# Gate rows made by transposing repeated columns, a new order of the first units, nine warm-up products, and a delta-rule inverse in 64-column tiles

## The reference

```python
def gated_delta_rule(q, k, v, g, beta):      # chunks of 64 tokens
    gc = jnp.cumsum(g, axis=-1)
    decay = jnp.exp(jnp.where(incl, gc[..., :, None] - gc[..., None, :], -jnp.inf))
    kb = k * beta
    low = jnp.where(strict, jnp.einsum("bhnid,bhnjd->bhnij", kb, k) * decay, 0.0)
    rhs = jnp.concatenate([v * beta, kb * jnp.exp(gc)[..., None]], axis=-1)
    sol = lax.linalg.triangular_solve(low + jnp.eye(c), rhs, left_side=True, lower=True, unit_diagonal=True)
...
def _fox_attention(q, k, v, f_pre):
    cum = jnp.cumsum(jax.nn.log_sigmoid(f_pre).transpose(0, 2, 1), axis=-1)
...
    s = s + (cqc[..., None] - cum[:, :, None, :])
```

## Time and profile before

| | us |
|---|---|
| median of three runs | 1081.33 (1081.12 to 1082.15) |
| the profiled execution, its own time | 1081.43 |
| its span in the trace | 1079.6 |
| PE busy | 1051.2 (97%) |
| DVE busy | 756.2 (70%) |
| ACT busy | 542.3 (50%) |
| POOL busy | 12.6 (1%) |

### The profile page before, as it was taken

How to read it: one execution, slowest core, us unless ns; L and a number is a source line. 1 busy time by engine, 2 the same in 40 slices (tenths; PEclk the granted TensorE clock), 3 DMA queues, 4 the chain that set the end, 5 groups by cost and what they waited for, 6 DMA issues and landing times.

```text
span 1079.6 us, 19214 instructions
## 1 busy us (share of the span) xinstructions
PE 1051.2 (97%) x7938; PEld 932.7 (86%) x7938; DVE 756.2 (70%) x1051; ACT 542.3 (50%) x601; POOL 12.6 (1%) x13
## 2 busy tenths in 40 slices
PE   9999999999999999999999999989999989999998
PEld 7999999999976798989899877659986659999986
DVE  6989947678458767677777856857797765556535
ACT  5675534563353463547536334576677654353331
POOL 0100000000000000000000000002000000000000
PEclk8999999999999999999999999999999999999999
DMA  8454432334325663425343354776344364545441
GB/s 343 157 180 155 157 118 90 138 125 159 115 79 213 252 239 155 132 104 193 121 157 118 118 200 153 310 291 260 127 156 156 103 243 163 195 172 181 176 163 51
DMA packets 26293, 181.32 MB, mean 168 GB/s; under 512 B 3040, under 2 KB 3296, under 8 KB 4960
## 3 DMA queue, kind: packets, MB, share of 16 engines
q1 hardware_dynamic: 25056, 174.66, 44.1%
q10 hardware_dynamic: 1152, 5.45, 1.2%
HBM read 179.04 MB, written 1.05 MB: 167 GB/s over the span
## 4 chain that ended last, share of the span: by engine, by line
PE 89%; DVE 7%; ACT 2%; issue 1%; DMA 1%; ACTq 0%; DVEq 0%; SPq 0%
PE PS L912 86%; DVE WL L1778 1%; PE PS L1065 1%; PE PS L1143 1%; DVE X L1972 1%; DVE X L1971 1%; DMA RAW<-wst 1%; PE PS L1289 0%; DVE layer_ln L2083 0%; DVE STAT L1953 0%; DVE X L1952 0%; ACT block L1606 0%; DVE X L2264 0%; DVE XTL L1995 0%; DVE layer L2076 0%
## 5 line engine op out<-in xcount | busy, mean ns | idle before, releaser
L912 PE MATMUL PS<-XTH,WH 128*128 128x256 f32 x1392 | 404.4, 291 | 0.7 <-issue 0.5
L912 PE MATMUL PS<-XTH,WL 128*128 128x256 f32 x1392 | 394.5, 283 | 0.0
L912 PE MATMUL PS<-XTL,WH 128*128 128x256 f32 x1392 | 394.4, 283 | 0.0
L1778 DVE TENSOR_TENSOR WL<-RAW,WH 128x2048 fp32r<-128x2048 f32 x138 | 316.9, 2297 | 107.9 <-ACT WH L1368 104.7
L1368 ACT ACTIVATE WH<-RAW 128x2048 fp32r<-128x2048 f32 x138 | 262.7, 1903 | 194.8 <-PE PS L912 191.2
L912 PEld LDWEIGHTS PS<-XTH,WH 128*128 128x128 f32 x1392 | 267.6, 192 | 6.3 <-issue 3.7
L912 PEld LDWEIGHTS PS<-XTL,WH 128*128 128x128 f32 x1392 | 267.7, 192 | 2.8 <-issue 2.6
L912 PEld LDWEIGHTS PS<-XTH,WL 128*128 128x128 f32 x1392 | 267.5, 192 | 0.0
L912 PE MATMUL PS<-WH,YH 128*128 128x512 f32 x224 | 89.6, 400 | 1.1 <-DVE YL L2256 1.1
L912 PE MATMUL PS<-WH,YL 128*128 128x512 f32 x224 | 87.4, 390 | 0.0
L912 PE MATMUL PS<-WL,YH 128*128 128x512 f32 x224 | 87.3, 390 | 0.0
(11 more groups left out here) (295 smaller groups left out, 1178.0 us busy)
## 6 DMA issues: line engine op xcount, KB each, us to landing
RAW<-wst SPq DMA_DIRECT2D x162, 1024.0 KB, 4.9
LNW<-lnrow ACTq DMA_DIRECT2D x3, 1024.0 KB, 6.4
RAW<-wst SPq DMA_DIRECT2D x4, 512.0 KB, 4.8
layer<-xt SPq DMA_DIRECT2D x2, 512.0 KB, 5.8
XR<-x ACTq DMA_DIRECT2D x1, 1024.0 KB, 6.2
out<-X SPq DMA_DIRECT2D x4, 256.0 KB, 2.1
CST<-cst ACTq DMA_DIRECT2D x1, 640.0 KB, 8.9
PT<-pt SPq DMA_DIRECT2D x1, 512.0 KB, 5.6
```

Source lines behind the costliest of these rows:

```text
L912: return pe.matmul(o, lhsT, rhs, start=start, stop=stop)
L1778: tt(WL[:, i % RAW_RING, 0:n], RAW[:, i % RAW_RING, 0:n], as_float(WH[:, k % SPLIT_RING, 0:n]), ALU.subtract).then_inc(vector_done, 1)
```

## The change

1. `gt` is gone. A new step `gcc:g` on PE is the small product with `triu` alone, and DVE's `gcc:g` copies its eight columns to `GCOL`. `gc:g` on PE is now eight transposes of a column of `GCOL` repeated 128 times. `gcc:0` stands right behind `norm:k:0` and waits for DVE's `ba2`; `gcc:1` stands behind `ab:1:0` and claims bank 2.
2. `gsp` is gone. DVE's `gcol` also stores the cumulated columns (`GRC`), and `grow` is 12 and 8 transposes.
3. PE begins with nine warm-up products, `first:k:0:0` and `k:0:0`, and `ba` after them. ACT and DVE split x's first half ahead of the slab's top half.
4. `gp` and `gu` on levels 1 to 6 are two products of 64 output rows in the place of one of 128: 16 PE instructions for 8, in each of the 48 steps.

```diff
 ORDER_T = """
-ba first:k:0:0 k:0:0 first:k:0:1 k:0:1 first:v:0:0 v:0:0 norm:k:0 first:v:0:1 v:0:1 first:q:0:0 q:0:0 first:q:0:1
+first:k:0:0 k:0:0 ba first:k:0:1 k:0:1 first:v:0:0 v:0:0 norm:k:0 gcc:0 first:v:0:1 v:0:1 first:q:0:0 q:0:0 first:q:0:1
...
-ab:1:0 first:zb:1:0 zb:1:0 gc:1 first:zb:1:1 first:ah:1:1 zb:1:1 vtr:1 norm:q:1 first:ac:1:1 ah:1:1 first:az:1:1
+ab:1:0 gcc:1 first:zb:1:0 zb:1:0 gc:1 first:zb:1:1 first:ah:1:1 zb:1:1 vtr:1 norm:q:1 first:ac:1:1 ah:1:1 first:az:1:1
...
-split_top xs:1 split:0:0 xs:0 ba split:1:1 split:2:2 ba1 k:0:0 split:3:3 k:0:1 split:4:4 v:0:0 split:5:5 ba2 norm:k:0
+xs:0 split_top xs:1 split:0:0 split:1:1 ba split:2:2 ba1 k:0:0 split:3:3 k:0:1 split:4:4 v:0:0 split:5:5 ba2 norm:k:0
...
+            def t_gcc(step, g):
+                pe.wait_ge(vector_done, vector_at("ba2"))
+                pe.wait_ge(cst_loaded, 16)
+                mm(PS[:, 2, 0:8], triu, GG[:, g, :]).then_inc(tensor_done, 1)
+
+            def repeated(o, column):
+
+                return pe.transpose(o, column.to_broadcast([P, P]), ident)
+
             def t_gc(step, g):
-                pe.wait_ge(vector_done, vector_at("ba2"))
-                pe.wait_ge(gpsimd_done, gpsimd_at("gt", g))
-                pe.wait_ge(cst_loaded, 16)
-                gt = flat(PM)
-                for i in range(2):
-                    mm(PS[:, i, :], ONES[:], gt[:, i * SLAB:(i + 1) * SLAB])
-                mm(PS[:, 2, 0:8], triu, GG[:, g, :]).then_inc(tensor_done, 1)
+                pe.wait_ge(vector_done, vector_at("gcc", g))
+                for m in range(NT * HG):
+                    last = repeated(PS[:, m // HG, m % HG * P:(m % HG + 1) * P], GCOL[:, m:m + 1])
+                last.then_inc(tensor_done, 1)
...
-                    last = mm(odd(PS[:, c, h * P:(h + 1) * P], i), DL[:, m, :], odd(U[:, m, :], i))
+                    for b in range(2):
+                        r = slice(b * HD, (b + 1) * HD)
+                        last = mm(odd(PS[r, c, h * P:(h + 1) * P], i), DL[:, m, r], odd(U[:, m, :], i))
...
             def t_grow(step, part):
-                pe.wait_ge(vector_done, vector_at("gsp"))
-                pe.wait_ge(gpsimd_done, gpsimd_at("gsp"))
+                pe.wait_ge(vector_done, vector_at("gcol"))
...
-                        o = a * T
-                        mm(PS[:, b, o:o + P], ONES[:], GSP[0][:, j, :])
-                        tot = NLS[:, 0, gate_of(j):gate_of(j) + 1].to_broadcast([P, P])
-                        mm(PS[:, b, o + P:o + T], ONES[:], tot, stop=False)
-                        last = mm(PS[:, b, o + P:o + T], ONES[:], GSP[1][:, j, :], start=False)
+                        for c in range(NT):
+                            o = a * T + c * P
+                            last = repeated(PS[:, b, o:o + P], GRC[:, c, j:j + 1])
...
-            for _ in range(6):
+            for _ in range(9):
                 mm(PS[:, 7, :], ONES[:], ONES[:].unsqueeze(1).to_broadcast([P, 4, P]))
```

More of the change, by code:

```diff
@@ L278, in gdn @@
     def gdn(g):
-        out = [later(step, "gt", g, on="G"),
-               later(step, "gc", g, on="TVS", banks=(0, 1, 2)),
+        out = [later(step, "gcc", g, on="TV", banks=(2,)),
+               later(step, "gc", g, on="TVS", banks=(0, 1)),
                later(step, "gc2", g, on="V"),
@@ L413, in plan @@
     root(0, 0)
-    step("gsp", on="GV")
     feat(2)
@@ L511 @@
 ORDER_S = """
-setup split_top xs:1 split:0:0 xs:0 split:1:1 ba1 split:2:2 split:3:3 k:0:0 split:4:4 k:0:1 split:5:5 ba2 norm:k:0
+setup xs:0 split_top xs:1 split:0:0 split:1:1 ba1 split:2:2 split:3:3 k:0:0 split:4:4 k:0:1 split:5:5 ba2 norm:k:0
 v:0:0 split:6:6 split:7:7 q:0:0 v:0:1 split:8:8 zb:0:0 q:0:1 split:9:9 split:10:10 zb:0:1 gc:0 split:11:11 norm:q:0
@@ L544 @@
 ORDER_V = """
-split_top xs:1 split:0:0 xs:0 ba split:1:1 split:2:2 ba1 k:0:0 split:3:3 k:0:1 split:4:4 v:0:0 split:5:5 ba2 norm:k:0
-split:6:6 q:0:0 split:7:7 v:0:1 q:0:1 split:8:8 gc:0 split:9:9 split:10:10 k:1:0 split:11:11 vtr:0 norm:q:0
+xs:0 split_top xs:1 split:0:0 split:1:1 ba split:2:2 ba1 k:0:0 split:3:3 k:0:1 split:4:4 v:0:0 split:5:5 ba2 norm:k:0
+split:6:6 q:0:0 gcc:0 split:7:7 v:0:1 q:0:1 split:8:8 gc:0 split:9:9 split:10:10 k:1:0 split:11:11 vtr:0 norm:q:0
 split:12:12 k:1:1 gc2:0 gk:0 split:14:14 split:13:13 gkk:0 v:1:0 gp:0:0:1 gp:0:0:0 split:15:15 gu:0:0:1 v:1:1
@@ L551 @@
 split:24:24 gp:0:6:1 ab:0:1 gks:0 gu:0:6:1 split:26:26 split:25:25 ac:1:0 split:27:27 gz:0 gr:0:0 split:28:28 ab:1:0
-gc:1 split:29:29 gc2:1 split:30:30 norm:q:1 vtr:1 gk:1 split:31:31 split:32:32 ac:1:1 gkk:1 split:33:33 ab:1:1
+gcc:1 gc:1 split:29:29 gc2:1 split:30:30 norm:q:1 vtr:1 gk:1 split:31:31 split:32:32 ac:1:1 gkk:1 split:33:33 ab:1:1
 gp:1:0:0 gp:1:0:1 gu:1:0:1 gu:1:0:0 split:34:34 gp:1:1:0 gp:1:1:1 gu:1:1:0 gp:1:2:0 split:35:35 gu:1:1:1 split:36:36
@@ L570 @@
 gate:1:1:1 rmsb:0:1 xt:4:3 xt:4:1 adat:7 xtl:4:2 xtl:4:0 xtl:4:3 xtl:4:1 adat:9 split:88:108 gates:0 split:89:109
-gates:1 ga gb split:90:110 gd split:91:111 qn:1:2 gcol gsp qn:0:0 split:92:112 qn:0:1 split:93:113 qn:0:2 split:95:115
+gates:1 ga gb split:90:110 gd split:91:111 qn:1:2 gcol qn:0:0 split:92:112 qn:0:1 split:93:113 qn:0:2 split:95:115
 split:94:114 feat:3 grow:0 split:96:116 feat:4 mod:1 grow:1 split:97:117 mb split:98:118 qn:1:0 gm score:0 qn:1:1
@@ L585 @@
 ORDER_G = """
-setup gt:0 gt:1 gsp
+setup
 """
@@ L1058, in t_gu @@
                     m = c * HG + h
-                    last = mm(odd(PS[:, 2 + c, h * P:(h + 1) * P], i), XI[:, m, :], odd(PM[:, m, :], i))
+                    for b in range(2):
+                        r = slice(b * HD, (b + 1) * HD)
+                        last = mm(odd(PS[r, 2 + c, h * P:(h + 1) * P], i), XI[:, m, r], odd(PM[:, m, :], i))
                 last.then_inc(tensor_done, 1)
@@ L1839, in v_conv, with v_gcc @@
                 return part
+            def v_gcc(g):
+                dve.wait_ge(tensor_done, tensor_at("gcc", g))
+                if g:
+                    dve.wait_ge(scalar_done, scalar_at("gc", 0))
+                    dve.wait_ge(tensor_done, tensor_at("gc", 0))
+                dve.tensor_copy(GCOL, PS[:, 2, 0:8]).then_inc(vector_done, 1)
             def v_gc(g):
@@ L2316, in g_setup @@
                 pool.memset(EPS[:, 1:2], L2_EPS).then_inc(gpsimd_done, 1)
[L2318 to L2335, removed]
+            parts = {"setup": g_setup}
             mine = 0
```

23 lines of the change are left out of this document (7 added, 16 removed).

## The result

| | before | after |
|---|---|---|
| median, us | 1081.34 (1081.12 to 1082.15) | 1100.75 (1099.76 to 1100.99) |
| ratio, 95% interval | 1 | 1.0176 (1.0159 to 1.0194) |
| span of the profiled execution | 1079.6 | 1099.2 |
| mean granted clock of PE | 0.995 | 0.984 |

What follows compares the result with a forecast made beforehand. PE, busy 1051.2 of 1079.6 us, and its waits were taken as the bound. +10.8 - 0.9 + 4.4 - 4.5 - 4.4 - 0.9 + 3.4 = +7.9 on 1081.43 gave 1089.3 us, range 1083 to 1096.

Steps and rivals of the forecast that it cites:

- The rival in which the waits are covered: ba2 ends before PE is through norm:k:0 and gr:0:0 before 212.1: sum -13.2, 1068 us; chance 0.06.
- the one with one wait: Start as worked out, gcc:1 covered, inverse at its full 13 us, without the clock: -4.9, 1076.5 us; chance 0.05.
- The waits of gc:1: At gcc:1, PE stands 5.3 us for DVE's gr:0:0, less 0.9 for shorter gc:1: +4.4 us.
- The clock: Half speed for 3.4 us after the stands at 31 to 44 us and after 217.4: +3.4 us, bounds 0 and 4.0.
- The start: ba behind the first unit delays DVE and ACT; PE stands at norm:k:0 and gcc:0 for ba2: +10.8 us.
- gc: Four instructions of 512 columns become eight transposes: -0.9 us each for gc:0 and gc:1.
- The inverse: Tiles of 64 output rows shorten the 48 steps: -4.5 us in group 0, -4.4 us in group 1.
- The rule that a change of tiling drains the engine: Some 27 runs of tiles each paying a product's 0.28 us: 4 to 5 us more, near 1094; only part of the slow rival (0.13).
- grow: Fewer instructions save PE 4.3 us, but score:0 waits for DVE's qn:1:0: -0.9 us, bounds 0 and 4.3.

Runs made afterwards that it cites:

- filler run: Kernel after plus products of ones that nobody reads in PE's four stands (norm:k:0, gcc:0, gcc:1, gc:1): 1094.10 us, ratio 1.0115.
- all three placements: Kernel after with the old start, gcc:0 one half unit ahead of gc:0, gcc:1 behind zb:1:0 and copied by DVE ahead of ab:1:0: 1073.47 us.

## Why the prediction was off, point by point

- **Direction and places: right.** PE stands ahead of `norm:k:0`, `gcc:0` and `gcc:1`, ended by what was named. The stand ahead of `gc:1` was not forecast. The rival in which the waits are covered and the one with one wait are refuted by the stands in the trace of after.
- **The waits of gc:1: the step that failed.** "The units queued behind it don't need the columns" looked only at PE's queue. Where the change puts DVE's own `gcc:1` was not followed: behind `ab:1:0`, in a chain through ACT back to PE's late unit. It cost 4.3 us of stand and 2.0 to 2.8 of clock behind it, more than half of the 11.6 us missed; with the copy moved alone, 6.9 us came back. The order of DVE in the change showed it.
- **The clock: right in kind, mis-sized.** One half-speed stretch of 3.4 us for each of two places was forecast, 3.4 us in all, bounded at 4.0. There were three behind stands, each of 4 to 6 us of full work, and the filler run puts them at 7.1 us. The lengths of 3.4 and 4.0 us, and with them the bound, were those of the two stretches of the earlier trace rows, and neither of these stood behind a long stand.
- **The start: +12.5 forecast with its clock, +14.3 measured.** The chain was right in every link, and too short by 2 us: the first unit came at 11.1 and not at 10.4, since about three more of the early warm-up instructions ran at 0.85 us than in the kernel before; `ba` took 4.2 us and not 3.5; DVE's `ba` began at 21.7 and not at 19.8. The same 2 us stand in `k:0:0` (27.86, forecast 25.9) and in the end of `ba2` (46.3, forecast 44.4).
- **gc: right,** -1.1 for -0.9.
- **The inverse: near in group 0 by luck** (4.2 for 4.5), **too large in group 1** (3.5 for 4.4). The forecast for group 0 was 0.3 us saved in each of 24 steps, 12 rows of steps at 0.1 us each and 1.5 us of waits. Measured were 0.43 us per step, 15 rows at 0.34 and about 1.0 us of waits: 10.3 - 5.1 - 1.0 = 4.2, so the errors cancel. In group 1 the sum had no term for the 11 changes of form; in the level of the earlier trace rows the waiting was 0.3 us, as forecast, and the two changes to transposes and back cost 0.25 us each. The tiles alone gave the same 3.6, so it was no disturbance from ahead. The rule that a change of tiling drains the engine (the Trainium skill, TensorEngine Tiling (Array Packing), Key Properties) was set aside because `hm` didn't show it. The trace agrees with it in direction, with 0.34 us per row of steps, which is more than the 0.28 us of a product that the prediction priced and dropped. `hm` does show it, on the way in, where the prediction looked only at the way out: its first tile starts at 413.55 us, 0.21 us behind the product ahead of it.

```profile
413.34 0.28 PE L912 MATMUL PS<-XTH,WL 128*128 128x256 f32 x1
```

- **grow: the waiting right (-1.1 for -0.9), the clock behind it not seen.** A stand of 2.1 us made of a gain a zero.

## What to carry to other kernels

When a small step is split off and placed early, follow it on every engine that has a part in it: what stands in front of it there, and whether that waits for the engine you are serving. Place a step that waits just ahead of its user, with cover in between, not where its inputs might be ready. A stand of PE ahead of full work can cost more than its length: the stands of 5.5, 5.0 and 4.3 us here cost 2.0 to 2.8 us of clock on top. If one can't be removed, products that nobody reads take that back. Put steps on smaller tiles back to back: alone between full products one gained 0.1 us here, each further one behind it 0.43.

## What the runs showed of the hardware that I had not expected

- Behind the stands of 4.3 to 5.5 us the next 4.1 to 5.8 us of full work ran at 0.50. Shorter stands did it in some kernels: one of 3.1 us ahead of `norm:k:0` but not those of 3.2 to 3.6 us at the same place, and one of 2.1 us ahead of `score:0`. The Trainium skill (TensorE: Matmul & The Clock Gate, What's actually happening) says that activity releases the throttle; the run with filler products agrees, with 1.00 behind every stand.
- PE can be busy throughout and still lose its clock: with `ba`, 32 instructions of 16 columns back to back from 17.2 to 21.4 us, the clock read 0.50 from 20.4 to 26.0 us. Four products of 256 columns strewn into it at the start kept 1.00, in both kernels that had them; the 0.7 us of idle time ahead of the first unit went with them.
- The first warm-up instructions of 512 columns go at 0.85 us each and the later ones at 0.43, read from the starts of their weight loads, while the granted clock is shown as 1.00. The pace changed at 4.3 us in the kernel before and at 6.3 in the kernel after, whose first products are the same: so the first unit can't be placed to better than 1 us. The traces' records of the clock begin at 3.9 and 6.3 us, about where the pace changes; the 1.00 shown for the time ahead of that has no record behind it, and the pace there is that of half clock.
- Where a half-speed stretch falls in a thin stage moves the end by about 1 us in either direction, in kernels that are alike there: among those with all three placements one has such a stretch at 713 us, three have it near 617 us, and one has neither. Differences under 2 us between such kernels say little.
